# A mixture-of-experts trunk on one core: the last expert's rows added on TensorE from chip memory, and small tables stored from ScalarE's queue

## What is computed

```python
h = rmsnorm(x, norm_ffn)
g_sel = argmax(h @ w_group + b_group)                    # 4 groups
top_p, top_i = top_k(softmax(e_logits[rows, g_sel]), 2)  # 2 of the 8 experts of the group
for each expert e, for its rows:                         # 32 experts, 1024 (token, choice) pairs
    ys = (silu(h @ w1[e]) * (h @ w3[e])) @ w2[e]         # 1024 -> 512 -> 1024
x = x + sum over the token's two choices of weight * ys
out = rmsnorm(x, final_norm)
```

## Time and profile before

| | |
|---|---|
| Median of three runs | 1352.01 us |
| The profiled execution's own time | 1348.63 us |
| Its span, first to last recorded instruction | 1346.6 us |
| TensorE busy / VectorE / ScalarE / GpSimd | 90% / 40% / 30% / 7% of the span |
| Mean granted TensorE clock | 0.982 of full speed |
| Read from device memory | 290.21 MB, 225 GB/s over the span |

### The profile page before, as it was taken

The page is one execution under the profiler, slowest core; times in us unless marked ns, Lnnn a source line. Parts: engine busy times, 40 slices in busy tenths (PEclk is TensorE's granted clock), DMA queues, the critical chain, the costliest instruction groups (busy, mean ns, idle before and its releaser), DMA issues. The chain is left out here.

```text
span 1346.6 us, 15473 instructions
## 1 busy us (share of the span) xinstructions
PE 1209.3 (90%) x6094; PEld 802.2 (60%) x6094; DVE 533.8 (40%) x980; ACT 405.5 (30%) x675; POOL 94.9 (7%) x126
## 2 busy tenths in 40 slices
PE   6999999999999999999998796999787897877784
PEld 5887877686778788888887674333333333333331
DVE  5324454568767348745445656110010010000014
ACT  5234443344543442244244421121111111111112
POOL 2000000000000000000000002211111111111100
PEclk9999999999999999999999995999999999999997
DMA  7222213212022212343423645899999999999995
GB/s 275 100 89 82 95 64 104 95 64 78 32 74 92 94 71 95 117 156 102 160 68 126 277 181 206 301 411 409 416 420 415 413 393 412 418 415 417 413 410 211
DMA packets 49436, 295.25 MB, mean 219 GB/s; under 512 B 8711, under 2 KB 8983, under 8 KB 20053
## 3 DMA queue, kind: packets, MB, share of 16 engines
q1 hardware_dynamic: 40340, 273.48, 52.0%
q0 software_dynamic: 8448, 18.69, 4.2%
q10 hardware_dynamic: 576, 2.10, 0.4%
HBM read 290.21 MB, written 12.93 MB: 225 GB/s over the span
## 5 line engine op out<-in xcount | busy, mean ns | idle before, releaser
L1825 PE MATMUL e_u<-w_raw,xT 128*64 128x512 f32 x1056 | 242.5, 605 | 58.8 <-DMA w_raw<-in_w 55.8
L1825 PEld LDWEIGHTS e_u<-w_raw,xT 128*64 128x64 f32 x1056 | 81.4, 139 | 215.6 <-issue 212.0
L2166 DVE SCALAR_TENSOR_TENSOR tn<-tn,e_u 64x512 f32<-64x512 f32 x33 | 22.4, 679 | 425.2 <-ACT tn L2067 425.2
L280 DVE TENSOR_TENSOR s_lo<-s_raw,s_hi 128x2048 fp32r<-128x2048 f32 (+1 forms) x68 | 138.5, 2037 | 56.4 <-ACT s_hi L275 55.7
L275 ACT CAST s_hi<-s_raw 128x2048 fp32r<-128x2048 f32 (+1 forms) x68 | 115.9, 1705 | 111.4 <-PE pz L594 41.1
L1835 PE MATMUL e_y<-w_raw,hidT 128*64 128x512 f32 x528 | 120.6, 598 | 15.4 <-ACT hidT L2062 15.4
L562 PE MATMUL pz<-hT_hi,s_hi 128*128 128x512 f32 x288 | 115.8, 402 | 0.0
L562 PE MATMUL pz<-hT_hi,s_lo 128*128 128x512 f32 x288 | 112.4, 390 | 0.0
L562 PE MATMUL pz<-hT_lo,s_hi 128*128 128x512 f32 x288 | 112.3, 390 | 0.0
L2057 ACT COPY xT<-e_x 128x512 f32<-128x512 f32 x33 | 19.3, 585 | 304.7 <-PE e_x L1810 304.7
L578 PE MATMUL pz<-hT_hi,s_hi 128*128 128x512 f32 x256 | 102.3, 399 | 0.5
(11 more groups left out here) (378 smaller groups left out, 1876.6 us busy)
## 6 DMA issues: line engine op xcount, KB each, us to landing
w_raw<-in_w SPq DMA_DIRECT2D x192, 1024.0 KB, 27.6
s_raw<-in_w_mix SPq DMA_DIRECT2D x30, 1024.0 KB, 4.9
s_raw<-in_w_gb SPq DMA_DIRECT2D x32, 768.0 KB, 4.3
s_raw<-in_w_out_pieces SPq DMA_DIRECT2D x4, 1024.0 KB, 4.9
w_raw<-ys_scratch SPq DMA_DIRECT2D x8, 512.0 KB, 7.3
x_sb<-in_x SPq DMA_DIRECT2D x4, 512.0 KB, 4.8
rel_bias<-in_rel_tiles POOLq DMA_DIRECT2D x8, 256.0 KB, 3.1
decay<-in_decay POOLq DMA_DIRECT2D x8, 256.0 KB, 4.3
```

The costliest lines, as they stand in the source:

```text
L280: nc.vector.tensor_tensor(w_lo[n % 2][:, 0:w], w_raw[n % 2][:, 0:w], w_hi[n % 2][:, 0:w].bitcast(F32), ALU.subtract).then_inc(w_split, 1)
L1825: m = nc.tensor.matmul(ps_u[o][lo:lo + FIRST, :], xT[b][:, k * FIRST:(k + 1) * FIRST], raw[j][:, kk * FF:(kk + 1) * FF], start=k == 0, sto ...
L2166: nc.vector.scalar_tensor_tensor(tn[:], tn[:], 1.0, ps_u[b][0:FIRST, :], ALU.add, ALU.mult).then_inc(s_hm, 1)
```

## The change

Five things are changed.

1. The stores of `jobsi` and `permi` move from SyncE's queue to ScalarE's, behind its first copy of turned rows (`tables_out`). ScalarE also stores `wsel` to a new scratch tensor, one float per row of `ys_scratch`: two transfers of 128 x 4 single elements.
2. The last turn's rows (expert 31) are not scattered to `ys_scratch` any more. In turn 4 GpSimd writes zeros to the rows of that expert (`f_zero`), and gathers the weight of each row of the expert (`w_last`).
3. SyncE issues the eight loads when the stores of all turns but the last have landed. It also loads the numbers 0 to 511 into every partition (`tokens`), behind the final gain.
4. VectorE makes a matrix `hot_last` of 128 x 512 from `tokens`: in the column of the token of a row stands the row's weight, elsewhere zero. Both halves of the partitions hold the same 64 rows' indices.
5. TensorE now sums all four tiles: for tiles 0 and 1 `x_sb`, to which VectorE has added the loaded rows, and the last expert's rows by `hot_last`; for tiles 2 and 3 also the loaded rows by diagonal matrices. `ps_x` and `ps_h` move into one tensor of two banks, and the sums take all eight banks. ScalarE and VectorE read every tile from there.

The core of the diff:

```diff
@@ -133,2 +133,3 @@
 jobs_dram = nc.dram_tensor("jobs_scratch", [1, P], I32).ap()
+wsel_dram = nc.dram_tensor("wsel_scratch", [SLOTS, 1], F32).ap()

@@ -1741,7 +1742,8 @@
     early = few("early", [P, 1])
-    weight_diag = Area(after_stats, top - 8 * KB_ - after_stats)("weight_diag", [P, 2, P])
-    ps_x, ps_h = psum(c, "e_x", (P, KD * FIRST)), psum(c, "e_h", (P, KF * FIRST))
-    ps_last = psum(c, "e_u", (P, D))
-    ps_u = [ps_last[:, b * FF:(b + 1) * FF] for b in range(2)]
-    ps_y = [psum(c, f"e_y{b}") for b in range(2)]
+    ids_last, tok_last, w_last = few("ids_last", [P, 1], U32), few("tok_last", [P, 1]), few("w_last", [P, 1])
+    weight_diag = Area(after_stats, top - 8 * KB_ - after_stats)("weight_diag", [P, 2, 2, P])
+    ps_xh, ps_uu, ps_yy, ps_f = (psum(c, "e_" + n, (P, D)) for n in ("xh", "u", "y", "f"))
+    ps_x, ps_h = ps_xh[:, 0:KD * FIRST], ps_xh[:, BW:BW + KF * FIRST]
+    ps_u, ps_y = ([o[:, b * FF:(b + 1) * FF] for b in range(2)] for o in (ps_uu, ps_yy))
+    summed = [ps_f, ps_uu, ps_xh, ps_yy]
     ys_halves = ys_dram.rearrange("s (h d) -> (s h) d", h=2)
@@ -1773,3 +1776,5 @@
         sem("f_" + n) for n in ("x", "ss", "ms", "sq", "o", "done", "gain", "diag", "last"))
-    END = [p for p in ORDER if AT[p] >= AT[ORDER[-1]] + 1 - DEPTH][:T + 1]
+    f_ids, f_wout, f_w, f_zero, f_tokens, f_hot = (
+        sem("f_" + n) for n in ("ids", "weights_out", "weights", "zero", "tokens", "hot"))
+    END = [p for p in ORDER if AT[p] >= AT[ORDER[-1]] + 1 - DEPTH][:T + 2]

@@ -1806,2 +1811,4 @@
     final_gain = raw[SLOT[END[T]]][:, D:2 * D]
+    tokens = raw[SLOT[END[T + 1]]][:, 0:N]
+    hot_last = nc.alloc_sbuf_tensor_at("hot_last", [P, N], F32, offset=raw_at[SLOT[END[T + 1]]] + N * 4)

@@ -1855,6 +1862,2 @@
         ring(known)
-        sp.wait_ge(s_jobs, 1)
-        sp.dma_start(jobs_dram[0:1, 0:4 * (JOBS + 1)].rearrange("o (j q) -> (o j) q", q=4),
-                     jobsi[0:JOBS + 1, :]).then_inc(s_jobs_out, 16)
-        sp.dma_start(jobs_dram[0:1, PERM_AT:PERM_AT + EXPERTS], permi[0:1, :]).then_inc(s_jobs_out, 16)
         sp.wait_ge(s_jobs_out, 32)
@@ -1879,4 +1882,6 @@
         sp.dma_start(final_gain, bass.AP(a["rows"].tensor, 0, [[0, P], [1, D]])).then_inc(f_gain, 16)
+        sp.dma_start(tokens, bass.AP(a["rows"].tensor, ROWS + D, [[0, P], [1, N]])).then_inc(f_tokens, 16)
+        sp.wait_ge(f_zero, 16)
         for b in range(2):
-            sp.wait_ge(s_ys[b], 16 * ((TURNS + 1 - b) // 2))
+            sp.wait_ge(s_ys[b], 16 * ((LAST + 1 - b) // 2))
         for t in range(T):
@@ -1916,2 +1922,4 @@
         nc.gpsimd.memset(xo[:], 0.0).then_inc(o_zero, 1)
+        nc.gpsimd.memset(yoo[:], 0.0).then_inc(o_zero, 1)
+        nc.gpsimd.memset(w_last[:], 0.0).then_inc(o_zero, 1)
         for ch in range(2):
@@ -1936,2 +1944,11 @@
                 store(q - 1)
+            if q == LIST_AT // 2:
+                pool.wait_ge(o_zero, 3)
+                pool.wait_ge(f_ids, 1)
+                pool.indirect_dma_start(ys_halves, bass.IndirectOffsetOnAxis(idy2[:, EXPERTS - 1:EXPERTS], 0),
+                                        yoo[:], None, bounds_check=last_y, oob_is_err=False).then_inc(f_zero, 16)
+                pool.wait_ge(f_wout, 16 * 2)
+                pool.indirect_dma_start(w_last[:], None, wsel_dram, bass.IndirectOffsetOnAxis(ids_last[:], 0),
+                                        bounds_check=last_w, oob_is_err=False).then_inc(f_w, 16)
+                pool.wait_ge(f_zero, 16)
             if q == LIST_AT:
@@ -1965,5 +1982,4 @@
                 store(q - 1)
-        store(LAST)
         for b in range(2):
-            pool.wait_ge(s_ys[b], 16 * ((TURNS + 1 - b) // 2))
+            pool.wait_ge(s_ys[b], 16 * ((LAST + 1 - b) // 2))

@@ -2038,14 +2054,24 @@
         experts(JOB + 1, TURNS)
-        pe.wait_ge(s_hd, TURNS)
-        for half in range(2):
-            nc.tensor.matmul(ps_u[half], ident[:], x_sb[:, T - 1, half * FF:(half + 1) * FF],
-                             start=True, stop=False)
-        pe.wait_ge(f_diag, 2)
-        for ch in range(2):
-            pe.wait_ge(f_ld[ch][T - 1], 16)
+        pe.wait_ge(f_hot, 1)
+        pe.wait_ge(s_yo, TURNS)
+        for t in range(T):
+            if t < 2:
+                pe.wait_ge(f_x, t + 1)
+            else:
+                pe.wait_ge(f_diag, 4)
+            o = [summed[t][:, half * FF:(half + 1) * FF] for half in range(2)]
             for half in range(2):
-                last = nc.tensor.matmul(ps_u[half], weight_diag[:, ch, :],
-                                        y_of(T - 1, ch)[:, half * FF:(half + 1) * FF],
-                                        start=False, stop=ch == 1)
-        last.then_inc(f_last, 1)
+                nc.tensor.matmul(o[half], ident[:], x_sb[:, t, half * FF:(half + 1) * FF],
+                                 start=True, stop=False)
+            for half in range(2):
+                at = slice(half * FIRST, (half + 1) * FIRST)
+                last = nc.tensor.matmul(o[half], hot_last[at, t * P:(t + 1) * P], yo[LAST % 2][at, :],
+                                        start=False, stop=t < 2)
+            for ch in range(2 * (t >= 2)):
+                pe.wait_ge(f_ld[ch][t], 16)
+                for half in range(2):
+                    last = nc.tensor.matmul(o[half], weight_diag[:, t - 2, ch, :],
+                                            y_of(t, ch)[:, half * FF:(half + 1) * FF],
+                                            start=False, stop=ch == 1)
+            last.then_inc(f_last, 1)

@@ -2073,3 +2099,12 @@
             wait(act, s_ys[q % 2], 16 * (q // 2))
-            nc.scalar.copy(yo[q % 2][:], ps_y[q % 2][:]).then_inc(s_yo, 1)
+            nc.scalar.copy(yo[q % 2][:], ps_y[q % 2]).then_inc(s_yo, 1)
+
+        def tables_out():
+            act.wait_ge(s_jobs, 1)
+            act.dma_start(jobs_dram[0:1, 0:4 * (JOBS + 1)].rearrange("o (j q) -> (o j) q", q=4),
+                          jobsi[0:JOBS + 1, :]).then_inc(s_jobs_out, 16)
+            act.dma_start(jobs_dram[0:1, PERM_AT:PERM_AT + EXPERTS], permi[0:1, :]).then_inc(s_jobs_out, 16)
+            for ch in range(2):
+                act.dma_start(wsel_dram[ch * N:(ch + 1) * N, :].rearrange("(t p) o -> p (t o)", p=P),
+                              wsel[:, ch, :], allow_slow_non_contiguous=True).then_inc(f_wout, 16)

@@ -2077,2 +2112,4 @@
             rows_in(lo)
+            if lo == 0:
+                tables_out()
             for q in range(lo, hi):
@@ -2107,9 +2144,4 @@
         for t in range(T):
-            if t < T - 1:
-                act.wait_ge(f_x, t + 1)
-                summed = x_sb[:, t, :]
-            else:
-                act.wait_ge(f_last, 1)
-                summed = ps_last[:]
-            nc.scalar.activation(junk, summed, ACT.Square, accum_out=ss[:, t:t + 1]).then_inc(f_ss, 1)
+            act.wait_ge(f_last, t + 1)
+            nc.scalar.activation(junk, summed[t][:], ACT.Square, accum_out=ss[:, t:t + 1]).then_inc(f_ss, 1)
             act.wait_ge(f_ms, t + 1)
@@ -2160,2 +2192,4 @@
         nc.vector.tensor_tensor(idx2[:], idf[:], here[:], ALU.add).then_inc(s_swap, 1)
+        nc.vector.tensor_tensor(tok_last[:], idf[:, EXPERTS - 1:EXPERTS], here[:, EXPERTS - 1:EXPERTS], ALU.add)
+        nc.vector.tensor_copy(ids_last[:], idf[:, EXPERTS - 1:EXPERTS]).then_inc(f_ids, 1)

@@ -2197,5 +2231,10 @@

-        for ch in range(2):
-            nc.vector.tensor_scalar(weight_diag[:, ch, :], ident[:], wsel[:, ch, T - 1:T], None, ALU.mult
-                                    ).then_inc(f_diag, 1)
+        for t in range(2):
+            for ch in range(2):
+                nc.vector.tensor_scalar(weight_diag[:, t, ch, :], ident[:], wsel[:, ch, 2 + t:3 + t], None,
+                                        ALU.mult).then_inc(f_diag, 1)
+        dve.wait_ge(f_w, 16)
+        dve.wait_ge(f_tokens, 16)
+        nc.vector.tensor_scalar(hot_last[:], tokens, tok_last[:], w_last[:], ALU.is_equal, ALU.mult
+                                ).then_inc(f_hot, 1)

@@ -2224,5 +2262,3 @@
         sums(1)
-        scale(0)
-        sums(2)
-        for t in range(1, T):
+        for t in range(T):
             scale(t)
```

24 lines of the change are left out of this document (13 added, 11 removed).

## The result

The changed kernel takes **1365.64 us** (median of 4 runs, 1362.09 to 1368.98) against 1351.59 (1349.95 to 1353.69, 4 runs) on the same chip: ratio 1.0111, interval 1.0084 to 1.0138. It is 14 us slower by the medians and 15.0 by the ratio, which counts from here on; that is far outside the range 1346.5 to 1354.2. The profiled execution was the longest of the four, with a span of 1366.9 us, and that of before, with 1348.63 us and a span of 1346.6, shorter than any of its four; so the spans differ by 20.3 us, more than the medians.

A forecast was written before the change was run, and what follows sets the result against it. The prediction took the transfer of 192 pieces of 1 MB to bound the experts' stage. Stream -4.9 and tail +3.3 gave -1.6 us, so 1350.4 us against 1352.01, range 1346.5 to 1354.2.

The forecast's parts named there:

- What bounds it: Experts' stage: bound by transferring 192 pieces of 1 MB; whatever the steady stream loses is paid at its end.
- The tables: Start of the experts' stage: storing both tables from ScalarE lets SyncE issue pieces earlier; 5.7 us gained, bounds 0 and 7.3.
- the hole: Low transfer rates from 855 to 870 us, between two batches of pieces: 2.38 MB lacking, 5.7 us at 417 GB/s.
- The store of `wsel`: ScalarE's queue, early in the experts' stage: 1024 elements of 4 bytes add 0.5 us to the stream, bounds 0.1 and 2.
- Rival (b): Start of the stream: the hole stays, tables landing late or elements holding ScalarE or the queues; +3.3, 1355.4 us; chance 0.1.
- The zeros: GpSimd's turn 4: one scatter of zeros, at most 0.26 MB, adds 0.3 us to the stream.
- ScalarE and GpSimd: Early turns: ScalarE's four extra issues and GpSimd's wait and memsets fit into free time; cost zero, 2 us without cover.
- The tail: After the last `down`: loads start 4.73 us earlier, but TensorE becomes the bound with 40 slots and a lower clock; +3.3 us.
- Rival (c): Tail: TensorE's clock stays up over the idle 4.9 us or recovers early; -3.4, 1348.6 us; chance 0.15.
- rival (d): Tail: TensorE's 64-partition pairs run one behind the other; 3.4 us more, 1353.8 us; chance 0.1.
- The signs to watch: Stream start and tail: short table wait, over 380 GB/s, earlier last matmuls, TensorE's sum 19 us; wrong if VectorE awaits `tokens`.
- The sum: Whole kernel: stream -4.9 and tail +3.3 make -1.6 us, forecast 1350.4 us; chance 0.45.

The follow-up runs named there:

- e6: The changed kernel with the two element-wise stores of `wsel` issued two turns later, at turn 2: 1366.3 us, ratio 1.011 to the kernel before.
- e1: The kernel before with only the stores of the two tables moved to ScalarE's queue: 1348.36 us, ratio 0.998 to the kernel before.
- e2: The kernel before with only the two element-wise stores of `wsel` added on ScalarE's queue: 1361.89 us, ratio 1.0076 to the kernel before.
- e9: e4 plus two stores of 512 four-byte elements each to a spare tensor, one element in each 64 bytes: 1357.12 us.
- e14: e4 plus one store of 128 four-byte elements at a pitch of 8 bytes to a spare tensor: 1357.27 us.
- e15: e4 plus one store of 128 four-byte elements at a pitch of 32 bytes to a spare tensor: 1354.79 us.
- e11: e4 plus one store of 128 four-byte elements side by side to a spare tensor: 1363.88 us.
- e4: The changed kernel with `wsel` stored as 128 pieces of 32 bytes and the gather's indices worked out for that order: 1355.31 us, ratio 1.0029 to before.
- e7: e3 with two element-wise loads of 512 four-byte elements each in place of the `wsel` stores: 1355.25 us, ratio 1.0026 to the kernel before.
- e3: The changed kernel without the `wsel` stores and the gather of the last expert's weights: 1354.69 us, ratio 1.0028 to the kernel before.

## Why the prediction was wrong

**What bounds it** held: wherever the stream stopped, the time was paid at the end, be it at 850 (the change) or at 875 (e6).

**The tables** did what they were said to do: SyncE's wait is gone and the hole closes. The size was put at -5.7 (0 to -7.3). e1 measures -2.7 (-4.3 to -1.1), and in its trace the stage is 479.1 instead of 483.0 us, -3.9. From 840 to 870 us e1 moves 339 GB/s for 262, which is 2.3 MB or 5.5 us at 417, as predicted; what becomes of the other 1.6 us I can't assign to a row; from 870 to 1300 the stream of e1 averages 413 GB/s for 414, which would be 1 us but is the last digit. The rule from the Trainium skill, "DMA: Bandwidth & Descriptors", "Issuing engines are not separate DMA queues", gave 0.6 us at most; e1's interval lies outside that, since what the move saves is a wait and not an issue.

**The store of `wsel`** is the step that failed: "I take 0.5 and 2 us as the upper one", priced by scatters of 128 elements each that ran in a stretch with a share of 0.02. Measured by difference it is 11.2 us, 10.3 in e2, 11.5 by the stretches of e6: the term of 0.5 us was off by 10.7, its upper bound by some 9. The scatters looked like the nearest row and were not: they write single elements too, but from GpSimd's queue, and to places picked by an index over 80 KB of lists. That they landed in 2.3 us said nothing of 512 elements side by side. I let the nearest row set the upper bound, although the transfer had no row of its kind at all, so that no row bounded it from above. (The flag `allow_slow_non_contiguous` in its call is no guide: e9, e14 and e15 bear it and lose little or nothing, e11 does without and loses 9.3 us.) The Trainium skill, "DMA: Bandwidth & Descriptors", "Rules for kernel authors", says that a strided last dimension becomes one descriptor per element and is to be rearranged. The advice is right here by 11 us (e4), but the count of descriptors isn't the reason: e7 loads as many elements and costs nothing measurable, and e11 loses 9.3 us with 128. By the same page's "Specifications" a transfer below 512 bytes is read, modified and written; the pieces of e9 and e15 have 4 bytes like those of e11 and lose little or nothing, so that alone doesn't explain it either.

**Rival (b)** had the right mechanism in half a sentence, "the 1024 elements hold ScalarE and the queues", and the right sign, but only as a way to keep the hole open, at no more than the hole's price. ScalarE was not held (0.95 us for both issues); the 16 engines were, and with them the gather issued behind, whose rows TensorE had only 19 us later. That made the hole larger than before. It had 0.1.

**The zeros** and the rest of the stream: e3's stage is 480.0 us (833.16 to 1313.16) against e1's 479.1, +0.9 with 0.3 predicted. **ScalarE and GpSimd** lost nothing on the path: `up(1)` starts 1.8 us after the turning of its rows begins (847.53 and 849.30), as before (844.50 and 846.27), and GpSimd's wait for its zeros took 4.8 us, once, and delayed no store: the next one followed after 12.5 us, as in the other turns.

**The tail** was put at +3.3 and is +6.7 in the trace, +6.5 by e3 and e1. The mechanism is right: TensorE becomes the bound and idles long enough for the clock to fall. Three sizes are off. TensorE starts 9.3 us after the last `down` did, where 8.6 was worked out: the loads came 3.1 us after their store and not 2.4. A tile's kinds of matmul don't follow one another without a seam: tile 3 took 6.57 us and not 6.0, the pair over 64 partitions alone 1.06 and not 0.86; over four tiles 1.5 us. And the clock cost 3.0 us, not 1.8: 3.68 for 1.86, 2.01 for 1.06 and 2.09 for 1.86 us. Together 3.4. Rival (c) falls, since the clock went down; rival (d) would have shown pairs of 1.7 us, and they took 1.06.

**The signs to watch**: the wait is gone (seen); over 380 GB/s from 855 to 870 (not seen: 249, 138 and 338); the last weights' matmuls 4 to 6 us earlier (not seen: the last `down` came 13.6 us later); TensorE's sum within 16 to 22 us (21.9, just inside). The last one, VectorE waiting for `tokens`, came true to the letter: it stood idle for 4.69 us until 1332.17. It cost nothing, since the loads that VectorE needs next let it go only at 1336.06; as a sign of error it was badly chosen.

**The sum** -4.9 + 3.3 = -1.6 reads in runs -2.7 + 11.2 + 6.5 = +15.0 us, which adds up by construction, since the terms are differences of the same runs. Of the 16.6 us between the two the stores of `wsel` have 10.7, the tables 3.0, the tail with the zeros 2.9.

## What to carry to other kernels

A transfer of a kind that no row shows has no upper bound from rows that merely look like it: measure it alone first. Store small per-partition data as one piece per partition and do the index arithmetic where it is read; the four small operations cost nothing measurable here, the element stores 11 us. When an engine takes over work in a tail, put what needs no load first: the same matmuls in another order were worth 10 us (8.6 in the traces), of which the clock that never fell was 2.2 against e4 (its first eight records took 3.68 and 1.48 us, for 1.86 and 1.06 at the full clock).
